# The last feed-forward of an fp32 kernel: both parts of the activation in one 512-column matmul

## The reference, cut to what matters

```
def swiglu_2(h, w_gate, w_up, w_down):
    return (jax.nn.silu(h @ w_gate) * (h @ w_up)) @ w_down
...
        h = modulate(rms_norm_2(x, ffn2_norm[l]), sh3, sc3)
        x = x + 0.5 * g3[:, None, :] * swiglu_2(h, ffn2_w_gate[l], ffn2_w_up[l], ffn2_w_down[l])
    return rms_norm_2(x, final_norm)
```

## Time and profile before

| | us |
|---|---|
| median of three runs | 1244.28 |
| lowest, highest | 1243.93, 1245.1 |
| the profiled execution, its own time | 1245.95 |
| its span in the trace | 1244.1 |
| PE busy | 1150.2 (92%) |
| DVE busy | 933.0 (75%) |
| ACT busy | 584.8 (47%) |
| mean granted clock of TensorE | 0.967 |

### The profile page before, as it was taken

The page is one execution under the profiler, slowest core; times in us unless marked ns, Lnnn a source line. Parts: engine busy times, 40 slices in busy tenths (PEclk is TensorE's granted clock), DMA queues, the critical chain, the costliest instruction groups (busy, mean ns, idle before and its releaser), DMA issues.

```text
span 1244.1 us, 19935 instructions
## 1 busy us (share of the span) xinstructions
PE 1150.2 (92%) x8342; PEld 1046.7 (84%) x8342; DVE 933.0 (75%) x1630; ACT 584.8 (47%) x960; POOL 74.5 (6%) x106
## 2 busy tenths in 40 slices
PE   2697898999998998899999999999989979999996
PEld 1695578999997996799999889999979967999996
DVE  5888858888776966788888688887666867765545
ACT  1434755443455457634444554444443355444433
POOL 1000000000000000186000000000000000000000
PEclk8799899999998998999999999999989999999999
DMA  9993234788982951477798447789622542765730
GB/s 374 360 381 139 117 136 179 305 328 280 336 317 100 379 213 41 148 288 263 310 261 333 184 178 289 284 245 353 263 107 97 109 178 101 265 249 193 180 131 34
DMA packets 40809, 280.75 MB, mean 226 GB/s; under 512 B 4736, under 2 KB 5264, under 8 KB 7952
## 3 DMA queue, kind: packets, MB, share of 16 engines
q1 hardware_dynamic: 37296, 269.27, 59.3%
q0 software_dynamic: 2416, 7.92, 2.1%
q10 hardware_dynamic: 1008, 2.30, 0.5%
HBM read 277.85 MB, written 1.10 MB: 224 GB/s over the span
## 4 chain that ended last, share of the span: by engine, by line
PE 68%; DVE 19%; DMA 6%; ACT 6%; issue 1%; ACTq 0%; SPq 0%; DVEq 0%
PE PS L413 68%; DMA raw<-WS 6%; DVE LO L1371 5%; DVE raw L1361 4%; ACT HI L952 2%; DVE TMP L1471 1%; DVE SC L1575 1%; ACT SQ L952 1%; DVE TMP L1436 1%; ACT HH L952 1%; ACT SC L952 1%; DVE SC L1560 1%; DVE HLo L1431 0%; PE PS L617 0%; DVE RS L1575 0%
## 5 line engine op out<-in xcount | busy, mean ns | idle before, releaser
L413 PE MATMUL PS<-HH,HI 128*128 128x256 f32 x1748 | 502.3, 287 | 27.7 <-ACT HH L952 24.9
L413 PE MATMUL PS<-HLo,HI 128*128 128x256 f32 x1748 | 503.9, 288 | 0.2
L413 PE MATMUL PS<-HH,LO 128*128 128x256 f32 x1748 | 500.5, 286 | 0.0
L1371 DVE TENSOR_TENSOR LO<-raw,HI 128x1024 fp32r<-128x1024 f32 x340 | 403.9, 1226 | 106.0 <-ACT HI L952 105.9
L952 ACT ACTIVATE HI<-raw 128x1024 fp32r<-128x1024 f32 x340 | 339.6, 1048 | 96.5 <-PE PS L413 58.7
L413 PEld LDWEIGHTS PS<-HH,HI 128*128 128x128 f32 x1748 | 341.2, 195 | 36.0 <-DVE LO L1371 20.5
L413 PEld LDWEIGHTS PS<-HH,LO 128*128 128x128 f32 x1748 | 341.1, 195 | 2.9
L413 PEld LDWEIGHTS PS<-HLo,HI 128*128 128x128 f32 x1748 | 340.5, 195 | 2.8 <-DVE HLo L1431 1.6
L1361 DVE CUSTOM_DVE_ANT_0 raw<-raw,CB,SM 128x1024 f32<-128x1024 f32 x168 | 210.6, 1285 | 23.1 <-DMA raw<-WS 23.0
L413 PE MATMUL PS<-HI,HDH 128*128 128x512 f32 x352 | 140.2, 398 | 0.0
L413 PE MATMUL PS<-HI,HDL 128*128 128x512 f32 x352 | 139.5, 396 | 0.0
(11 more groups left out here) (235 smaller groups left out, 1008.2 us busy)
## 6 DMA issues: line engine op xcount, KB each, us to landing
raw<-WS SPq DMA_DIRECT2D x255, 1024.0 KB, 5.3
SC<-scratch POOLq DMA_DIRECT2D x2, 1024.0 KB, 16.1
FB<-gates_out POOLq DMA_DIRECT2D x3, 512.0 KB, 5.1
SQ<-gates_out POOLq DMA_DIRECT2D x3, 512.0 KB, 9.6
X<-xT ACTq DMA_DIRECT2D x1, 1024.0 KB, 6.8
SC<-ssm POOLq DMA_DIRECT2D x2, 512.0 KB, 4.3
out<-TMP SPq DMA_DIRECT2D x2, 512.0 KB, 2.6
CB<-vecs SPq DMA_DIRECT2D x1, 512.0 KB, 6.5
```

The costliest lines, as they stand in the source:

```text
L413: return e.matmul(o, l, r, start=start, stop=stop, skip_group_check=True)
L1371: e.tensor_tensor(LO[:, s % HL, :], raw_half(j, h), HI[:, s % HL, :].bitcast(fp32), O.subtract).then_inc(*D.up(("lo", s)))
```

## The change

For j = 1 to 21 of f3 only (WIDE), the parts HH and HLo become two halves of one tile HB, at the places where they were. One matmul with the high weights takes both parts of block k as its moving operand, 2 x 256 columns that lie 2048 elements (8 KB) apart, and writes a whole bank: high W x high h in columns 0 to 255, high W x low h in columns 256 to 511. A second matmul, with the low weights, adds low W x high h to columns 0 to 255. So a half takes 8 x 2 matmuls where it took 8 x 3, and a bank of its own, two for a j.

The two column ranges of a bank then have to be added. ACT copies the upper range into SIL (gate) or HF (up), DVE adds the lower range from the bank (and frees the bank), ACT makes the silu of SIL in place, DVE multiplies HF by it in place. The work of PE on the gate half is signalled by itself, so ACT and DVE can start on it while PE is on the up half. DVE waits for its own last write before the product and behind it.

```diff
--- before.py
+++ after.py
@@ -9,6 +9,7 @@
 RAW, HL, AHEAD = 5, 6, 4
 COLS, HALF = 2048, 1024
 WORK0, NWORK = 4, 4
+WIDE = ("f3",)
 LNEXP = "natural_log_exp_and_others"
 
 
@@ -219,8 +220,8 @@
         X = sb("X", [128, 2, 1024])
         TMP = sb("TMP", [128, 8, 256])
         SQ = sb("SQ", [128, 8, 256])
-        HH = sb("HH", [128, 8, 256], f32r)
-        HLo = sb("HLo", [128, 8, 256], f32r)
+        HB = sb("HB", [128, 2, 8, 256], f32r)
+        HH, HLo = HB[:, 0], HB[:, 1]
         nones = sb("nones", [128, 128])
         zeros = sb("zeros", [128, 128])
         zb = zeros[:, :].bitcast(mybir.dt.bfloat16)
@@ -562,7 +563,8 @@
 
                 for j in range(22):
                     key = (tag, "in", j)
-                    ps = take((key, 0))
+                    wide = tag in WIDE and j > 0
+                    pair = [take((key, g)) for g in range(2)] if wide else [take((key, 0))] * 2
                     wt = [[x.rearrange("p (k n) -> p k n", k=8) for x in weight(key, 0)]]
                     if j == 0:
                         wt.append([x.rearrange("p (k n) -> p k n", k=8) for x in weight(key, 1)])
@@ -572,15 +574,21 @@
                     for g, k in turns:
                         if len(wt) == g:
                             wt.append([x.rearrange("p (k n) -> p k n", k=8) for x in weight(key, 1)])
-                        i = mm3(ps[:, g * 256:(g + 1) * 256], [x[:, k, :] for x in wt[g]], H2[k], k,
-                                g == 0 and k == 0, k == 7, tag)
+                        if wide:
+                            mm(pair[g].rearrange("p (c n) -> p c n", c=2), wt[g][0][:, k, :], HB[:, :, k, :], k == 0,
+                               k == 7)
+                            i = mm(pair[g][:, 0:256], wt[g][1][:, k, :], HH[:, k, :], False, k == 7)
+                        else:
+                            i = mm3(pair[g][:, g * 256:(g + 1) * 256], [x[:, k, :] for x in wt[g]], H2[k], k,
+                                    g == 0 and k == 0, k == 7, tag)
                         if k == 7:
-                            i.then_inc(*P.up(("in", tag, j), used(key, g)))
+                            i.then_inc(*P.up(("in", tag, j, g), used(key, g)))
                     walk.catch_up(walk.unit - 1, 1)
                     slow(j)
                     if j == 12:
                         mods(gcol + 8)
-                    banks.give((key, 0))
+                    for g in range(2 if wide else 1):
+                        banks.give((key, g))
                     if j > 1:
                         down(j - 2)
                 key = (tag, "dn", 10)
@@ -1066,8 +1074,18 @@
                     slow(j)
                     if j > 1:
                         w.wait_ge(*D.at(("hf", tag, j - 2)))
-                    w.wait_ge(*P.at(("in", tag, j)))
-                    fn(SIL[:, j % 2, :], bank((key, 0))[:, 0:256], F.Silu).then_inc(*A.up(("sil", tag, j)))
+                    if tag in WIDE and j > 0:
+                        w.wait_ge(*P.at(("in", tag, j, 0)))
+                        fn(SIL[:, j % 2, :], bank((key, 0))[:, 256:512], F.Copy).then_inc(*A.up(("part", tag, j, 0)))
+                        w.wait_ge(*D.at(("sum", tag, j, 0)))
+                        fn(SIL[:, j % 2, :], SIL[:, j % 2, :], F.Silu).then_inc(*A.up(("sil", tag, j)))
+                        w.wait_ge(*P.at(("in", tag, j, 1)))
+                        if j > 1:
+                            w.wait_ge(*D.at(("hdl", tag, j - 2)))
+                        fn(HF[:, j % 2, :], bank((key, 1))[:, 256:512], F.Copy).then_inc(*A.up(("part", tag, j, 1)))
+                    else:
+                        w.wait_ge(*P.at(("in", tag, j, 1)))
+                        fn(SIL[:, j % 2, :], bank((key, 0))[:, 0:256], F.Silu).then_inc(*A.up(("sil", tag, j)))
                     if j == 21:
                         e.preload_act_table_set(LNEXP)
                     w.wait_ge(*D.at(("hf", tag, j)))
@@ -1528,9 +1546,20 @@
                         mods(row[0] + 8)
                     for _ in range(steps):
                         next(later, None)
-                    w.wait_ge(*A.at(("sil", tag, j)))
-                    e.tensor_tensor(HF[:, j % 2, :], SIL[:, j % 2, :], bank((key, 0))[:, 256:512], O.mult) \
-                        .then_inc(*D.up(("hf", tag, j), ("free", (key, 0))))
+                    if tag in WIDE and j > 0:
+                        for g, o in enumerate((SIL[:, j % 2, :], HF[:, j % 2, :])):
+                            w.wait_ge(*A.at(("part", tag, j, g)))
+                            e.tensor_tensor(o, o, bank((key, g))[:, 0:256], O.add) \
+                                .then_inc(*D.up(("free", (key, g)), ("sum", tag, j, g)))
+                        w.wait_ge(*A.at(("sil", tag, j)))
+                        w.wait_ge(*D.now())
+                        e.tensor_tensor(HF[:, j % 2, :], HF[:, j % 2, :], SIL[:, j % 2, :], O.mult) \
+                            .then_inc(*D.up(("hf", tag, j)))
+                        w.wait_ge(*D.now())
+                    else:
+                        w.wait_ge(*A.at(("sil", tag, j)))
+                        e.tensor_tensor(HF[:, j % 2, :], SIL[:, j % 2, :], bank((key, 0))[:, 256:512], O.mult) \
+                            .then_inc(*D.up(("hf", tag, j), ("free", (key, 0))))
                     w.wait_ge(*A.at(("hdh", tag, j)))
                     e.tensor_tensor(HDL[:, j % 3, :], HF[:, j % 2, :], HDH[:, j % 3, :].bitcast(fp32), O.subtract) \
                         .then_inc(*D.up(("hdl", tag, j)))
```

## The result

The changed kernel takes 1242.12 us, against 1245.27 us for the kernel before on the same chip (medians of ten runs each): a ratio of 0.9975, interval 0.9966 to 0.9985, or 3.1 us less (1.9 to 4.2). The forecast was 3.1 us. Its absolute number, 1241.2, started from a median of three runs that lay 1.0 us lower than this one.

The account below looks back on a forecast made before the run. The prediction took PE's matmul pitch to bound f3. Step 1 saved 3.1 us and the other steps cost 0, so 1244.28 - 3.1 = 1241.2 us; pricing ends 1240.1 and 1242.4, range 1239.7 to 1244.8.

Parts of the forecast that it names:

- Step 1: PE in f3: 336 triples of 256-column matmuls become a 512- and a 256-column one, 9.2 ns saved each, 3.1 us.
- the prediction's own sign: Wide start to narrow start in f3: about 230 ns shows the forecast, 234 the first rival, over 239 the seam.
- first rival: PE's pitch in f3: fixed share at most 5.6 ns a matmul, 1.9 us or less gained; chance 0.22.
- The row taken: Last down matmul before in(3) of f3, 1066.13 to 1066.36 us, giving 230 ns for the wide matmul.
- Step 2: Added sums and copies on DVE and ACT in f3 stay hidden beside PE: cost 0, perhaps 0.5 us once.
- Step 3: Two banks a j in f3: sums free them in time for in(j+2), cost 0.
- Step 4: End of f3, j = 21: HDL at most 0.1 us later, still before PE needs it; cost 0.
- The seam: Wide matmul's two-piece operand in f3: rivals with an extra start, +1.1 us (chance 0.08) or +4.5 us (chance 0.07).
- The waits on LO: Rival: PE waits on LO in f3's iterations with modulation work, four places at 1 us, about 1245 us; chance 0.03.

Follow-up runs that it names:

- run with four and four: Changed kernel with PE's order altered in f3 to four wide matmuls, then four narrow ones, twice; ratio 0.9979 to the kernel before.
- first run: Changed kernel with only PE's merging undone, three 256-column matmuls again, two banks and the new ACT and DVE chain kept; ratio 0.9997 to the kernel before.
- second run: Changed kernel with the two parts of each block side by side, so the wide matmul reads 512 columns from one place; ratio 0.9969 to the kernel before.

## Why the prediction was right

**Step 1, the pitch.** The sum was right, its two terms were not. A pair was put at 230 + 119.6 = 349.6 ns and takes 349.9. But the wide matmul takes 233.8 ns and not 230, and the narrow one 116.1, not 119.6 (starts to next starts, averaged over some 300 pairs between 1060 and 1222 us). By the prediction's own sign, 234 ns from a wide start to the narrow one spoke for the first rival; the sign was a poor one, since only the pair's sum decides. The row taken, a 512-column matmul in front of a 256-column one, was the right neighbour for the pair, by some luck for each part. It was also one row read to 10 ns. Averaged over the 19 crossings of the kernel before, that step is 229.2 ns, and the step back, from the last 256-column matmul to the first 512-column one, is 120.9 and not the 130 of the single row; together 350.1, close to what the pair takes. With 233.6 + 119.6, the rival's pricing, the gain would have been 1.9 us; the rival's price for the wide one was nearly exact, and it failed on the narrow one, which is faster behind a wide one. The run with four and four bears this out: the narrow one behind a wide one takes 116.5 ns, one behind a narrow one 119.9. Why it is faster there no run shows. The first run shows that nothing else of the change moved the time. That the measured 3.1 us equals the forecast to the digit is partly luck: the stage shows 2.7 us in the traces, and the interval is wide.

The gap rule of the Trainium skill ("TensorE: Matmul & The Clock Gate", section "Back-to-back issue gap"), 2.5 ns for each matmul, which the page states for an isolated one, gives an estimate of 0.84 us. The traces have 359.1 - 349.9 = 9.2 ns for each matmul removed, and the measurement decides.

**Step 2, DVE and ACT.** Right in outcome, with the lead as foretold: at j = 1 the first LO behind the chain was to be ready 1.0 us ahead of in(3). DVE of the changed kernel:

```profile
1061.42 0.42 DVE L1564 TENSOR_TENSOR HDL<-FB,HDH 128x256 fp32r<-128x256 f32 x1 [0.56 <-ACT HDH L960]
...
1062.97 3.49 DVE L1389 TENSOR_TENSOR LO<-raw,HI 128x1024 fp32r<-128x1024 f32 x3
```

The first of the three ends at about 1064.1 and in(3) starts at 1065.26: 1.1 us. The price by volume, 0.84 us a j, was however no measure of the load on DVE: where DVE is late, and that is in 15 of the 21 wide j of f3 too, it stands 3.03 us in the chain, 1.7 more than before. Here that was hidden; in f0 to f2 it led to 72 us of waits and lower clock, and with 1.23 us more in f3 the cover is gone.

**Step 3, the banks.** No wait of PE on a sum in f3, and the first run has the two banks at no cost.

**Step 4, the end.** ACT, last iteration of the changed kernel, as the earlier trace rows:

```profile
1222.36 0.38 ACT L960 ACTIVATE FB<-PS 128x256 f32<-128x256 f32 x1 [1.54 <-PE PS L414]
1222.76 1.28 ACT L1090 ACT_TABLE_LOAD   x1
1224.06 0.42 ACT L960 ACTIVATE HDH<-FB 128x256 fp32r<-128x256 f32 x1
```

HDH starts 1.70 us after the copy, as it did after the silu (1227.84 - 1226.14 = 1.70). Sum and product fit beside the table load, and HDL starts 0.52 us behind HDH where it was 0.45.

**The rivals.** The seam costs nothing (second run). The waits on LO do not come in the changed kernel, but they were nearer than a chance of 0.03 says: 1.23 us a j bring them.

## What to carry to other kernels

Where PE is the bound, merging two 256-column matmuls with the same weights into one of 512 columns saves a fixed few nanoseconds each (9 here at the upper clock, nothing at the lower one), so count the matmuls, and take the pitch of the pair from a place where such a pair stands. What it costs an engine that takes its steps in the order of the program is not the added operations but the time it stands in the chain, pauses included: order the helper engine's steps so that what the other one needs next is ready (both copies ahead of the silu gave 38 us back where DVE was late). And judge the room by how early the result is when PE asks for it; the busy share hides the pauses.

## What the runs showed of the hardware

- The pitch of a 256-column fp32r matmul depends on its neighbours: 119.7 ns among its like, 116.1 between 512-column ones, at a granted clock of 1.00.
- At a granted clock of 0.5 three 256-column matmuls took 640 ns, and so did a 512-column one with a 256-column one; at 1.00 it was 359.1 against 349.9 ns. What a merged matmul saves was there at the upper level only.
- The pitch of 512-column ones was 226.6 ns with HH and HLo as weights, 233.9 with HDH and HDL, 232.2 after these had moved by 32 bytes, and 231.7 to 233.8 for the wide ones. What sets it was not found.
- Sixteen pairs take 5.55 and 5.64 us in turns from one j to the next, and a shift of other tiles by 32 bytes swaps the turns.
- A moving operand in two pieces 8 KB apart is as fast as one piece: 233.8 ns in both runs.
